# First block: one half of each later projection ahead of the head's r step, and the output gate projected ahead of the values

## The reference

```python
hn = rms_norm(h, norm1_g[i])
z = hn @ w_in[i]
qa, ka, va, qb, kb, vb, ob, ib, fb, uc, vc = split_cols(z, IN_SPLITS)   # 6 x 384, 384, 4, 4, 256, 256
ya = stick_breaking_attention(qa, ka, va)        # 6 heads of 64
ya = rms_norm(ya, sb_out_g[i])
qk = jax.nn.silu(causal_depthwise_conv(jnp.concatenate([qb, kb], axis=-1), conv_w[i], conv_b[i]))
hb = mlstm_chunkwise(qb, kb, vb, ib + igate_b[i], fb + fgate_b[i])       # 4 heads of 96
hb = rms_norm(hb, mnorm_g[i].reshape(ML_HEADS, ML_HEAD_DIM)).reshape(Bn, S, ML_WIDTH)
yb = hb * jax.nn.sigmoid(ob)
yc = spatial_gating(jax.nn.gelu(uc), jax.nn.gelu(vc), ...)
h = h + jnp.concatenate([ya, yb, rms_norm(yc, sgu_out_g[i])], axis=-1) @ w_out[i]
h = h + hierarchical_moe(rms_norm(h, norm2_g[i]), ...)                   # 32 experts, 2 per token
```

## Time and profile before

| | us |
|---|---|
| median of 3 runs | 1323.96 |
| lowest and highest | 1319.77 and 1328.98 |
| the profiled execution, own time | 1326.66 |
| its span in the profile | 1324.9 |
| TensorE busy in the span | 1147.2 (87%) |
| VectorE, ScalarE, GpSimd busy | 573.3, 244.1, 34.0 |
| mean granted TensorE clock | 0.928 of full speed |

### The profile page before, as it was taken

The page is one execution under the profiler, slowest core; times in us unless marked ns, Lnnn a source line. Parts: engine busy times, 40 slices in busy tenths (PEclk is TensorE's granted clock), DMA queues, the critical chain, the costliest instruction groups (busy, mean ns, idle before and its releaser), DMA issues.

```text
span 1324.9 us, 21110 instructions
## 1 busy us (share of the span) xinstructions
PE 1147.2 (87%) x7589; PEld 627.8 (47%) x7589; DVE 573.3 (43%) x1638; ACT 244.1 (18%) x510; POOL 34.0 (3%) x174
## 2 busy tenths in 40 slices
PE   6898899995665796999988998997999989979997
PEld 4655555542222345854444445643444534445434
DVE  3552537432222212899775626433233333323334
ACT  2022322110000224001235313111011111111111
POOL 1000100000000000000110001000000000000000
PEclk9898878998778897999999998999899989989989
DMA  9995548689999973354422455679989999999995
GB/s 328 381 343 220 192 155 317 263 346 421 421 420 422 386 240 127 128 190 141 176 90 101 150 193 207 240 302 428 425 335 427 422 414 428 426 414 423 426 406 204
DMA packets 87309, 399.97 MB, mean 302 GB/s; under 512 B 10646, under 2 KB 19352, under 8 KB 58544
## 3 DMA queue, kind: packets, MB, share of 16 engines
q1 hardware_dynamic: 86272, 398.15, 75.8%
q10 hardware_dynamic: 816, 0.52, 0.3%
q0 software_dynamic: 128, 0.03, 0.0%
HBM read 397.60 MB, written 1.07 MB: 301 GB/s over the span
## 4 chain that ended last, share of the span: by engine, by line
PE 46%; DMA 9%; DVE 3%; ACT 1%; SPq 1%; issue 1%; ACTq 1%; DVEq 0%
PE ps L2411 17%; PE ps L468 10%; PE ps L501 7%; DMA big<-in_w_exp_down 7%; PE ps L427 4%; PE ps L440 2%; PE ps L2447 2%; DMA ring<-in_w_exp_gu 2%; SPq L139 1%; SPq L144 1%; PE ps L417 0%; PE ps L487 0%; ACTq L1014 0%; DVE big L2207 0%; DVE big L2205 0%
## 5 line engine op out<-in xcount | busy, mean ns | idle before, releaser
L468 PE MATMUL ps<-ring,big 128*32 128x512 f32 x1936 | 259.1, 615 | 66.7 <-DMA ring<-in_w_up 45.8
L468 PEld LDWEIGHTS ps<-ring,big 128*32 128x32 f32 x1936 | 75.8, 114 | 204.0 <-issue 204.0
L501 PE MATMUL ps<-big 128*32 128x512 f32 x1120 | 140.2, 645 | 35.5 <-DMA big<-in_w_exp_down 28.1
L2411 PE MATMUL ps<-ring,big 128*128 128x512 f32 x320 | 139.7, 599 | 1.4 <-ACTq L1006 0.9
L468 PE MATMUL ps<-big 128*32 128x512 f32 x304 | 121.2, 623 | 0.0
L427 PEld LDWEIGHTS ps<-big 128*128 128x128 bf16 x1776 | 104.4, 98 | 30.0 <-issue 27.7
L427 PE MATMUL ps<-big 128*128 128x128 bf16 x1776 | 113.5, 219 | 1.4 <-ACT big L287 1.4
L2193 DVE SCALAR_TENSOR_TENSOR big<-big 128x256 f32<-128x256 f32 x240 | 105.6, 481 | 9.3 <-issue 0.4
L2411 PEld LDWEIGHTS ps<-ring,big 128*128 128x128 f32 x320 | 61.2, 192 | 78.1 <-issue 76.2
L501 PEld LDWEIGHTS ps<-big 128*32 128x32 f32 x1120 | 37.6, 117 | 110.9 <-issue 108.6
L287 ACT COPY big<-ps 128x512 f32<-128x512 f32 x74 | 43.4, 586 | 181.5 <-PE ps L427 181.5
(11 more groups left out here) (488 smaller groups left out, 1215.0 us busy)
## 6 DMA issues: line engine op xcount, KB each, us to landing
ring<-in_w_exp_gu SPq DMA_DIRECT2D x55, 2048.0 KB, 17.6
big<-in_w_exp_down SPq DMA_DIRECT2D x64, 1024.0 KB, 13.1
big<-in_w_down SPq DMA_DIRECT2D x32, 1024.0 KB, 18.3
ring<-in_w_in SPq DMA_DIRECT2D x15, 2048.0 KB, 9.0
ring<-in_w_gate SPq DMA_DIRECT2D x28, 1024.0 KB, 18.0
ring<-in_w_up SPq DMA_DIRECT2D x28, 1024.0 KB, 20.0
ring<-in_w_ada SPq DMA_DIRECT2D x12, 2048.0 KB, 16.6
big<-in_w_exp_gu SPq DMA_DIRECT2D x9, 2048.0 KB, 18.6
```

Source lines behind the costliest of these rows:

```text
L468: last = pe.matmul(ps[rows, BG, :], m.xsT[:, k, rows], m.gu(gu[j], k), start=(k == 0), stop=(k == KC - 1), skip_group_check=True)
L501: last = pe.matmul(ps[rows, BD + n, :], m.hidT[:, k, rows], m.dring[:, down[j], k * D + n * 512:k * D + n * 512 + 512], start=(k == 0), st ...
L2411: last = pe.matmul(bank, lhs(k), rhs(k), start=(k == 0 and start), stop=(k == kk - 1))
```

## The change

Three edits. The last two column blocks of `w_in` change places, so that the two tiles of `ob` are projected as i = 0, 1 (heads 0 and 1) and those of `vb` as i = 2, 3 (heads 2 to 4). The sigmoid's last two steps leave ML head 1 on VectorE and run by tile, 128 x 384, behind the convolution's taps of head 3 and behind the scans of head 4. And of each head's list of halves the first one goes to TensorE ahead of `sb_r(h)`, the rest stays behind it.

```diff
-                (1920, 384, 20, 0), (2304, 384, 22, 4))
+                (2304, 384, 20, 0), (1920, 384, 22, 4))
...
                     if i < TT:
+                        take(ob[:, t, :], lambda b: b[:, 0:MLW], ACT.Exp, scale=-1.0)
+                    else:
                         take(vba[:, t, :, 0:MLD], lambda b: b[:, 0:MLW].rearrange("p (h d) -> p h d", h=MLH))
-                    else:
-                        take(ob[:, t, :], lambda b: b[:, 0:MLW], ACT.Exp, scale=-1.0)
...
+                def output_gate(t):
+
+                    dve.wait_ge(ev("proj_evac"), 18 + t + 1)
+                    dve.tensor_scalar(ob[:, t, :], ob[:, t, :], 1.0, None, ALU.add)
+                    dve.drain()
+                    dve.reciprocal(ob[:, t, :], ob[:, t, :])
+
...
                         if h == CONV_K - 1:
                             last.then_inc(ev("conv"), 1)
+                    if h >= 3 and h - 3 < TT:
+                        output_gate(h - 3)
...
-                        dve.wait_ge(ev("proj_all"), 1)
-                        dve.tensor_scalar(ob, ob, 1.0, None, ALU.add)
-                        dve.drain()
-                        dve.reciprocal(ob, ob)
...
                     if h + 1 < SBH:
                         sb_z(h + 1)
+                    for i, half in LATER_HALVES[h][0:1]:
+                        later_projection(i, half)
                     sb_r(h)
-                    for i, half in LATER_HALVES[h]:
+                    for i, half in LATER_HALVES[h][1:]:
                         later_projection(i, half)
                     ada_steps(ADA_STEPS[h])
```

## The result

| | us |
|---|---|
| before, median of 5 runs | 1324.15 (1319.77 to 1328.98) |
| changed, median of 5 runs | 1315.92 (1314.78 to 1316.99) |
| ratio | 0.9928, 95% interval 0.9908 to 0.9948 |
| span of the profiled execution, before and changed | 1324.9 and 1314.2 |

The changed kernel is faster by 8.2 us by the medians, 9.5 us by the ratio, 10.7 us in the two profiled executions. In the listings of the changed kernel, lines behind the edits have moved: the projection is L1692 (was L1687), z L1756 and L1757, r L1763 to L1765, the ada matmuls L1740, y L1770 to L1772, the mixing L1833, the softplus L1494.

A forecast was written before the change was run, and what follows sets the result against it. In the heads TensorE was taken to idle at r for GpSimd's mask, at a price in clock too. 11.3 us earlier r(5) less 2.1 us low clock gives 9.2, gate and swap 0: median 1315, range 1307 to 1323.

The forecast's parts named there:

- The bound: In the six attention heads, TensorE waits 11.2 us for GpSimd's mask at r while independent projection work stands behind r.
- Heads 0 to 4: Halves ahead of r fill TensorE's waits: r(3) at 123.64 (was 133.33), r(4) at 131.67 (was 142.98).
- r(5): Hangs on r(4) by 8.96 us of ScalarE chain: comes at 140.63, 11.3 us earlier, with TensorE idle 4.5 us before it.
- The low clock: The 4.5 us gap before r(5) drops TensorE's clock for r(5) and the last 16 ada matmuls: 2.1 us charged.
- Rival B: Clock stays low from the r(5) gap to the mixing: 4.6 us beyond the charge, gain 4.6, time 1319; chance 0.15.
- The 5.3 us given back in heads 0 to 3: Low-clock losses of heads 0, 2 and 3 that go away, beside 6.0 us of idle, in the 11.3 us.
- The gate: VectorE's output gate moved from the ML stage to heads 3 and 4: 0 to 1 us loss, 0 gain.
- the cover named: The half in front of r(4) hides the gate's delay of head 4's softplus; without it, 1 us cost.
- The pass-through: Behind the heads everything is released by this chain, so the full DMA stretch starts earlier, unshortened, and the whole gain passes.
- Rival D: Gain absorbed in the DMA-full stretch if earlier loads, not `y_ready`, set its start: 1323; chance 0.13.
- The sum: 11.3 - 2.1 = 9.2 us gain: 1317.5 for the profiled execution, 1314.8 for the median, rounded 1315.
- Rival C: Gap costs nothing, or the 20 us at 0.50 behind the heads starts later: 2.1 to 7 more, 1306 to 1313; chance 0.12.

The follow-up runs named there:

- the half behind r(4): Whole change, but head 4's half of a projection stays behind r(4): 1312.76 us, ratio 0.9907 to the kernel before.
- the Silu block moved out of the chain: Whole change, with the convolution's Silu, its two table loads and three queue loads moved ahead of ScalarE's wait for r(4): 1310.26 us, ratio 0.9888.
- the three kernels that leave them as before: Kernel before; same with block swap and early gate alone, ratio 1.0004; same plus 10 one-column products at TensorE's start, ratio 1.0032.
- the filled ones: Kernel before plus unused products in idle time ahead of r, heads 0 to 3: ratio 0.9996, again 0.9999; with 54 one-column products more, 0.9975.
- a block moved behind its step: Whole change, with the convolution's Silu and its two table loads moved on ScalarE from ahead of Abs(5) to behind Exp(5): 1314.85 us, ratio 0.9919.

## Why the prediction was right, step by step

**The bound.** Right: the wait at r was the gap, and the move alone gives the gain (ratio 0.9932 alone, 0.9928 with the rest).

**Heads 0 to 4.** Right within 0.7 us, and always in the same direction: y(1) 110.54 for 111.03, y(2) 118.79 for 119.35, r(3) 123.02 for 123.64, r(4) 131.05 for 131.67. Of this, 0.16 us was there at z(0) already; the rest is about 0.1 us a head that I lost by adding pieces end to end, where the trace overlaps their ends with the next starts. The chains came as read: in front of r(2) the longer ScalarE chain still shows (0.28 us), in front of r(1) and r(3) nothing.

**r(5).** Right: 8.86 us behind r(4) for 8.96, TensorE idle 4.29 us for 4.5. That this part of the move stops paying is shown from both sides: counted from z(0), the half behind r(4) brings r(5) 2.5 us earlier, the Silu block moved out of the chain 4.2 us.

**The low clock.** Right in kind, and in size within what one execution differs from the next. Charged were 2.1 us behind the gap; found were 1.5 us (r(5) 12.0 us earlier than before, the mixing 10.5). With the same gap the kernel with the move alone took 12.8 us from r(5) to the mixing, the changed kernel 10.9 and the kernel before 9.3, so there it cost 3.5 us. Rival B did not come in the changed kernel: the clock was back by 144. The move alone went part of its way, low again from the ML scores on (two of their three larger pieces took 1.22 us there, 0.70 in the changed kernel). That the gap was the cause of the fall is shown by filling it, but filling it did not keep all of the 1.5 us, since the clock then fell a few us later, among the ML scores. The 5.3 us given back in heads 0 to 3 were what was left of 11.3 when the idle time was taken out; added up from the durations in the profile of before, what ran at the low clock there cost 5.6 us, and with the gaps filled it measured 5.6 in three traces. But all this is against one execution of the kernel before: the heads of the three kernels that leave them as before took 4.2, 5.6 and 8.8 us longer than the filled ones. That the execution on which the prediction rests lay between the other two is luck.

**The gate.** Right: neutral alone, ratio 1.0004. Its halves took 2.55 and 0.36 us each for 2.5 and 0.3; it delayed softplus(4) to 127.35, by 1.2 us (ScalarE's Ln ended at 126.17), under the cover named.

**The pass-through.** Right in the profiled executions: 10.5 us at the mixing, 10.5 at the issue of the router loads (182.06 for 192.56), 10.4 at the first round of the second block's experts, 10.7 at the end. Rival D did not come. The step is weaker than I put it: through the expert rounds of the second block the kernels here drift by about 3 us against one another, up and down again, so a gain of under 3 us need not show at the end. And an edit that changes the count of TensorE instructions can change the end by 3 us; this change leaves that count alone (7589 matmuls in both), which the prediction did not look at.

**The sum.** 1315 for 1315.92. Rival C's 17 us of TensorE work at the low clock read 18.9 in the earlier trace rows; the forecast does not use them. By parts the profiled execution gained 10.7 where 9.2 was forecast: 0.6 from the steps of the heads and r(5), 0.16 from before z(0), 0.6 from the clock charge, the rest unassigned. That the difference by the ratio, 9.5, lies nearer to the 9.2 than this does is luck: the profiled execution of before lay 2.5 us above the median, and the clock alone moved the heads by more than that between executions.

## What to carry to other kernels

Put independent work ahead of a step that waits, but only as far as the next chain allows: where the following step hangs on this one through another engine, work ahead of it delays that chain, and the idle time opens behind. Look for slack on the engine that holds the chain as well: a block moved behind its step only moved the wait, the same block ahead of it filled idle time. And before a gain is called lost, look whether the added instructions themselves made a stall far away.

## What the runs showed of the hardware that was not expected

Adding 16, 24 or 40 instructions to TensorE's program of some fifteen thousand changed a standstill some 1.2 to 1.3 ms later from 0.9 to 1.6 us into 3.0 to 3.3, and the last stretch by 3 us; adding 256 did not. Forty of them with no work worth naming cost 4.2 us by the runs. In the long standstills one packet of instructions was being fetched. The gap of 1.71 us in front of r(5) left the clock high in the kernel before and was followed by the low clock in the filled one (first piece 0.70 and 1.22 us), and the gap of 2.95 us in front of r(0) was followed by the low clock in two executions and left it high in a third (1.22, 1.22 and 0.70 us). So a gap of either size can go both ways, and a time taken from one trace with such gaps carries some us of chance.
